# A decoder trunk on one core: the last unit of each down projection by column halves over both tiles, and what is ordered around it

## The reference, cut to what matters

```python
def rms_norm(x, g):
    y = xf * lax.rsqrt(jnp.mean(xf * xf, axis=-1, keepdims=True) + NORM_EPS)
    return (y * g).astype(x.dtype)

def modulate(x, g, shift, scale):
    return rms_norm(x, g) * (1 + scale[:, None, :]) + shift[:, None, :]

hh = modulate(x, norm_g[l, 0], mod[:, 0], mod[:, 1])
x = x + 0.5 * mod[:, 2, None] * swiglu(hh, ffn_w_gu[l, 0], ffn_w_d[l, 0])
hh = modulate(x, norm_g[l, 1], mod[:, 3], mod[:, 4])
...                                    # rglru_mixer in layer 0, diff_attn_mixer in layer 1
x = x + mod[:, 5, None] * m
hh = modulate(x, norm_g[l, 2], mod[:, 6], mod[:, 7])
x = x + 0.5 * mod[:, 8, None] * swiglu(hh, ffn_w_gu[l, 1], ffn_w_d[l, 1])
...
y = rms_norm(x, final_g)
```

## Time and profile before

| what | value |
|---|---|
| three runs | 2417.99, 2424.96 and 2431.77 us |
| median | 2424.96 us |
| the profiled execution, its own time | 2418.17 us |
| its span, first to last instruction | 2416.4 us |
| mean granted TensorE clock | 0.991 |
| PE, DVE, ACT busy | 96%, 41%, 32% |
| chain that ended last | PE 83%, DVE 8%, issue 5%, ACT 3% |

### The profile page before, as it was taken

One profiled execution on the slowest core, in us unless ns is written; L12 is line 12 of the kernel. 1 busy time (PEld: TensorE's weight loads), 2 busy tenths in 40 slices (PEclk: granted clock), 3 DMA queues, 4 the chain that ended last, 5 costly groups with the idle time before them and its releaser, 6 DMA issues.

```text
span 2416.4 us, 42067 instructions
## 1 busy us (share of the span) xinstructions
PE 2322.3 (96%) x18402; PEld 2195.2 (91%) x18402; DVE 984.6 (41%) x1643; ACT 772.2 (32%) x1069; POOL 160.9 (7%) x133
## 2 busy tenths in 40 slices
PE   5999999999999999999999999999788899999998
PEld 4999999989899999999999999999544499999998
DVE  5222232488642322327452322327466553222325
ACT  4221212367442121225442122125344533212122
POOL 0100000000011010000001000010000101001010
PEclk9999999999999999999999999999899999999999
DMA  8432343212332432432532333214499432222221
GB/s 343 157 124 99 145 157 136 97 40 96 142 155 74 155 139 89 153 127 91 210 150 101 141 147 150 88 64 155 163 418 417 173 139 87 88 88 80 80 78 66
DMA packets 64553, 338.38 MB, mean 140 GB/s; under 512 B 8050, under 2 KB 12274, under 8 KB 34930
## 3 DMA queue, kind: packets, MB, share of 16 engines
q1 hardware_dynamic: 61426, 330.97, 36.0%
q10 hardware_dynamic: 2944, 4.72, 0.5%
HBM read 328.44 MB, written 7.23 MB: 139 GB/s over the span
## 4 chain that ended last, share of the span: by engine, by line
PE 83%; DVE 8%; issue 5%; ACT 3%; DMA 1%; POOL 0%; SPq 0%; ACTq 0%; DVEq 0%; POOLq 0%
PE ps L496 45%; PE ps L499 22%; PE ps L508 3%; PE ps L510 3%; PE ps L509 3%; PE ps L473 2%; DVE w_lo L1385 1%; PE ps L768 1%; DVE xc L1674 1%; PE ps L757 1%; PE ps L800 1%; ACT w_hi L881 1%; DVE hf L1420 0%; DVE hs L1717 0%; ACT nt L1229 0%
## 5 line engine op out<-in xcount | busy, mean ns | idle before, releaser
L496 PE MATMUL ps<-hh_hi,w_hi 128*128 128x288 f32 x2912 | 816.2, 295 | 1.6 <-DVE w_lo L1385 1.6
L496 PE MATMUL ps<-hh_lo,w_hi 128*128 128x288 f32 x2912 | 816.1, 295 | 0.0
L499 PE MATMUL ps<-hh_hi,w_lo 128*128 128x288 f32 x2912 | 617.0, 292 | 0.0
L496 PEld LDWEIGHTS ps<-hh_hi,w_hi 128*128 128x128 f32 x2912 | 546.2, 188 | 5.4 <-issue 3.3
L496 PEld LDWEIGHTS ps<-hh_lo,w_hi 128*128 128x128 f32 x2912 | 546.5, 188 | 0.4
L1385 DVE TENSOR_TENSOR w_lo<-raw,w_hi 128x2048 fp32r<-128x2048 f32 x164 | 375.9, 2292 | 304.6 <-ACT w_hi L881 281.7
L499 PEld LDWEIGHTS ps<-hh_hi,w_lo 128*128 128x128 f32 x2912 | 466.5, 188 | 0.0
L496 PE MATMUL ps<-h_lo,w_hi 128*128 128x288 f32 x1536 | 430.8, 295 | 0.0
L496 PE MATMUL ps<-h_hi,w_hi 128*128 128x288 f32 x1536 | 429.9, 295 | 0.7 <-DVE x L1565 0.7
L881 ACT ACTIVATE w_hi<-raw 128x2048 fp32r<-128x2048 f32 x159 | 303.4, 1908 | 332.0 <-PE ps L499 317.8
L499 PE MATMUL ps<-h_hi,w_lo 128*128 128x288 f32 x1536 | 325.5, 292 | 0.0
(11 more groups left out here) (224 smaller groups left out, 1957.3 us busy)
## 6 DMA issues: line engine op xcount, KB each, us to landing
raw<-in_w_gu SPq DMA_DIRECT2D x88, 1024.0 KB, 4.8
ada<-in_ada_w SPq DMA_DIRECT2D x76, 1024.0 KB, 10.8
raw<-in_w_d SPq DMA_DIRECT2D x32, 1024.0 KB, 4.8
kr<-in_k_cache SPq DMA_DIRECT2D x64, 512.0 KB, 7.8
vr<-in_v_cache SPq DMA_DIRECT2D x64, 512.0 KB, 8.3
raw<-in_w_d SPq DMA_DIRECT2D x16, 768.0 KB, 4.3
raw<-in_w_in SPq DMA_DIRECT2D x8, 1024.0 KB, 5.0
raw<-in_w_kv SPq DMA_DIRECT2D x8, 1024.0 KB, 4.9
```

The source lines that it names most:

```text
L496: pe.matmul(ps[:, 2 * s + n, 0:TH], whi, r[:, k, TH * n:TH * n + TH], start=(k == 0 and r is rhs_hi), stop=False)
L499: mm = pe.matmul(ps[:, 2 * s + n, 0:TH], wlo, rhs_hi[:, k, TH * n:TH * n + TH], start=False, stop=(k == k_tiles - 1))
```

## The change

The last unit goes by column halves over both tiles: (half 0, tile 0), (half 0, tile 1), (half 1, tile 0), (half 1, tile 1). The sums of half 0 (`acc_sums`, then `last_sums`) stand ahead of the last three products of (half 1, tile 0); those of half 1 move behind the `ada_burst` of the next stage. The squares of block 6 are made and added by halves (`square_six`, `add_six`). DVE's `last_unit` does the first 288 columns of both residuals, the rest of block 6, then two norm blocks of the next stage (`norm_start`) or two final rows, and only then the rest of block 7. The remaining norm blocks are `norm_rest`.

```diff
             def unit_with_sums(u, j, kt, st):
...
-                tile_products(j, 0, h_hi, h_lo, 0, kt, None, 0, "out0_full")
-                pe.wait_ge(sems["s1_free"], u + CREDITS["s1_free"])
                 for n in range(2):
-                    for k in range(kt):
-                        mm = part(j, 1, n, k, h_hi, h_lo, kt)
-                        if n == 1 and k == kt - 2:
-                            acc_sums(st)
-                    mm.then_inc(sems["w_done" if n else "half_full"], 1)
-                last_sums(st, 0)
+                    for t in range(2):
+                        if (n, t) == (0, 1):
+                            pe.wait_ge(sems["s1_free"], u + CREDITS["s1_free"])
+                        for k in range(kt):
+                            mm = part(j, t, n, k, h_hi, h_lo, kt)
+                            if (n, t, k) == (1, 0, kt - 2):
+                                acc_sums(st, 0)
+                                last_sums(st, 0)
+                        mm.then_inc(sems[("out0_full", "w_done")[t] if n else "half_full"], 1)
...
@@ first_unit and first_pair @@
+                acc_sums(sums, 1)
                 last_sums(sums, 1)
...
@@ ScalarE, behind the units of a down projection @@
-                        act.wait_ge(sems["res_half"], s["stat"])
+                        act.wait_ge(sems["res_half"], 2 * s["stat"] - 1)
+                        square_six(s["stat"], 0)
+                        act.wait_ge(sems["res_half"], 2 * s["stat"])
                         square_half(s["stat"], 0)
                         statistics(s["stat"], 0)
+                        act.wait_ge(sems["s0_free"], u0 + s["units"] + CREDITS["s0_free"])
+                        square_six(s["stat"], 1)
+                        if not s["last"]:
+                            norm_first(plan[at + 1], 0, False, range(2))
                         act.wait_ge(sems["s1_free"], u0 + s["units"] + CREDITS["s1_free"])
                         square_half(s["stat"], 1)
...
@@ VectorE @@
+            def add_six(st, n):
+
+                cols = slice(TH * n, TH * n + TH)
+                dve.wait_ge(sems["sq6_full"], 2 * st + n - 1)
+                dve.wait_ge(sems["sq_sum"], 8 * st + KT - 1)
+                dve.tensor_tensor(rstd[:, cols], rstd[:, cols], sg[0][:, cols], ALU.add)\
+                   .then_inc(sems["sq_sum" if n else "sq6_sum"], 1)
+
+            def last_unit(s, u, norm):
+
+                st, res = s["stat"], s["res"]
+                for t in range(2):
+                    residual_first(u, KT - 2 + t, t, "half_full", 2 * st - 1 + t).then_inc(sems["res_half"], 1)
+                    if t == 0:
+                        add_six(st, 0)
+                residual_second(u, KT - 2, 0, res + KT - 2)
+                add_six(st, 1)
+                if norm:
+                    norm_start(norm)
+                else:
+                    final_rows(s, 0, range(2))
+                residual_second(u, KT - 1, 1, res + KT - 1)
```

More of the change, by code:

```diff
@@ L632, in unit, with acc_sums @@
                     ada_turn(BURSTS[u])
[L634 to L638, removed]
+            def acc_sums(st, n):
+                if st and n == 0:
+                    pe.wait_ge(sems["sq6_sum"], st)
+                else:
+                    pe.wait_ge(sems["sq_sum"], 8 * st + 8)
+                pe.matmul(ps[:, 6 + n, 0:TH], ones, rstd[:, TH * n:TH * n + TH], start=True, stop=False)
             def last_sums(st, n):
@@ L656, in _ @@
             pe.wait_ge(sems["cond_ready"], 1)
-            acc_sums(0)
             for n in range(2):
+                acc_sums(0, n)
                 last_sums(0, n)
@@ L725, in _ @@
                     if s["last"]:
+                        acc_sums(s["stat"], 1)
                         last_sums(s["stat"], 1)
@@ L940, in norm_hi, with norm_first @@
                                bias=mods[:, s["sh"] + k, 0:1]).then_inc(sems["norm_hi"], 1)
-            def norm_first(s, sums, freed):
+            def norm_first(s, sums, freed, blocks=range(KT)):
                 act.wait_ge(sems["ada_evac"], s["sh"] // 8 + 1)
-                for k in range(KT):
+                for k in blocks:
                     if freed and k < KT - 1:
@@ L1434, in after_kv, with norm_start, norm_rest @@
                 return s["norm"] and plan[plan.index(s) - 1]["kind"] == "kv"
+            def norm_start(s):
+                dve.wait_ge(sems["h_lo"], s["h"] + CREDITS["h_lo"])
+                dve.wait_ge(sems["rstd_ready"], 2 * s["stat"] - 1)
+                for k in range(2):
+                    norm_gain(s, 0, k)
+                for k in range(2):
+                    norm_low(s, 0, k)
+            def norm_rest(s):
+                dve.wait_ge(sems["s1_free"], s["u"] + CREDITS["s1_free"])
+                for k in range(2, 4):
+                    norm_gain(s, 0, k)
+                for k in range(4, KT):
+                    dve.wait_ge(sems["norm_lo"], 16 * s["norm"] + k - 3)
+                    norm_gain(s, 0, k)
+                    norm_low(s, 0, k - 2)
+                for k in range(KT - 2, KT):
+                    norm_low(s, 0, k)
             def norm_first(s):
@@ L1600, in _ @@
                 if s["kind"] == "final":
[L1601 to L1606, removed]
+                    final_rows(plan[at - 1], 0, range(2, KT))
+                    final_rows(plan[at - 1], 1, range(KT))
                 if s["kind"] == "up":
@@ L1640, in _ @@
                             modulation(plan[at + 1])
[L1641 to L1645, removed]
+                        if s["sums"] and m == s["units"] - 1:
+                            last_unit(s, u, None if s["last"] else plan[at + 1])
+                        else:
+                            for t in range(2):
+                                k = 2 * m + t
+                                residual(u, k, t, s["res"] + k)
+                                if s["sums"]:
+                                    add_square(s["stat"], k)
                         if u in BURSTS:
```

44 lines of the change are left out of this document (29 added, 15 removed).

## The result

The changed kernel takes 2424.08 us (median of 12 runs, 2422.19 to 2433.52), the kernel before 2420.1 us on the same chip (median of 12, 2417.99 to 2431.77). The ratio is 1.0018, 95% interval [1.0009, 1.0026]: 2 to 6 us slower, inside the 0.5% that were called "no change". A second set of runs of the same kernel gave 1.0022 [1.0010, 1.0033]. The forecast was 2427.8 on the older median of 2424.96, +2.8 us (+0.12%); the measured ratio is +0.18%. That older median, of three runs, lay 4.9 us above the median of twelve, so the differences are to be compared and not the 2427.8 itself. (In the later sets of runs one execution of each kernel took far longer, 3853 and 7489 us; the ratios leave these two out.)

A forecast was written before the change was run, and what follows sets the result against it. The prediction took PE, busy for 96% of the span, to bound the kernel. Its terms 3.25 + 0.8 + 1.34 - 1.4 - 1.2 gave +2.8 us on the median 2424.96, so 2427.8 us, range 2416 to 2436.

The forecast's parts named there:

- Boundary 1, +3.25: First stage change: PE stops at half 0's sums, tile 1's release and the burst come later, half 1 starts 3.25 us later.
- the predicted 1.3: At boundary 1, a new PE stop of 1.3 us at the sums of half 0.
- Boundaries 3 and 4, +0.67 each: Stage changes 3 and 4: the new stop gives back the won `w_lo` wait; half 1 starts 0.67 us later at each.
- Boundaries 2 and 5, -0.7: Stage changes with `kt` 8: no stop at the sums, and PE passes the `w_lo` wait 0.7 us earlier at each.
- the end, -1.2: Boundary 6: two of 16 final rows made ahead of the last residual, the other 14 start sooner; end 1.2 us earlier.
- The clock, +0.8 (0 to 1.6) at boundary 1: A half-clock stretch of PE after the new idle time ahead of the burst, taken as 0.8 us, between 0 and 1.6.
- The price of 1.5: Cost in us of one slow clock stretch on PE: 15 products in 3.30 us instead of 25 at 0.130.
- A: Block 6's residual and sums are in time everywhere, as a step ahead on DVE ends sooner; -7 us, 2418; chance 0.13.
- B: New PE stops at boundaries 1, 3 and 4 each bring a slow clock stretch; +6.5 us, 2431.5; chance 0.22.
- C: Waiting early sums and the earlier norm cancel, also at boundary 1, ACT's Ln coming earlier; 0 to -1, 2424.5; chance 0.15.

The follow-up runs named there:

- e1: The changed kernel with the first unit's burst issued ahead of its waits for `w_lo`, `s0_free` and `s1_free`; 2420.2 us in one run.
- e2: The changed kernel with the sums of half 0 moved 15 products later on PE in units of 6 blocks, not the last; 2425.13 us in one run.
- e3: The changed kernel with DVE's next `w_lo` and modulation moved from ahead of the last unit's first residual to behind block 6's half add; 2425.71 us in one run.
- e4: The changed kernel without the two early norm blocks; the norm of half 0 begins behind tile 1's release; 2421.33 us in one run.
- e5: The changed kernel with the first unit's burst ahead of its waits, and `w_lo` and modulation behind block 6's half add; 2417.43 us (median of 11), ratio 0.9989.
- e8: The changed kernel as it is, run a second time; 2425.12 us (median of 12), ratio 1.0022.
- e9: The changed kernel without its two early final rows, all 16 standing behind the last residual; 2428.03 us in one run.
- e6: The kernel before, with the first unit's burst issued ahead of its waits for `w_lo`, `s0_free` and `s1_free`; 2418.37 us in one run.

## Why the prediction was right, and where its sizes failed

**Boundary 1, +3.25 (measured +3.36): right, step by step.** The stop is 1.14 in the bracket and 1.30 from where the next product would have started (478.73) to the sums at 480.03, which is how the predicted 1.3 was counted; the burst is +2.88 (+2.77). The runs with the changed order add up in one way. The shift of half 1 is the shift of the burst, plus 0.48 for the two passes of the sums that now stand behind it, plus what a slow stretch takes on the burst itself (its length less 3.66):

| kernel | idle ahead of the burst | burst | slow stretch on it | sum with 0.48 | half 1, measured |
|---|---|---|---|---|---|
| changed | 2.46 | +2.88 | 0 | 3.36 | +3.36 |
| e1 | 0 | +0.36 | 0 | 0.84 | +0.84 |
| e2 | 4.05 | +2.65 | 2.86 | 5.99 | +5.99 |
| e3 | 3.11 | +1.80 | 1.65 | 3.93 | +3.94 |
| e4 | 1.09 | +1.52 | 0 | 2.00 | +2.00 |
| e5 | 0 | -1.38 | 0 | -0.90 | -0.90 |
| e8 | 2.45 | +2.88 | 1.69 | 5.05 | +5.05 |
| e9 | 2.45 | +2.87 | 1.69 | 5.04 | +5.04 |

So what the change does here it does through one instruction's place: the burst, which needs nothing from tile 1, waits for its release (e1, e4).

**Boundaries 3 and 4, +0.67 each (measured +0.91 and +0.92): the mechanism right, the term small by a quarter.** I had PE and `w_lo` ready at the same moment, 1124.4. PE's side was nearly so: the parts of half 0 came 1.51 later (1.4 predicted). What was too small is the Ln that `w_lo` follows, +0.65 in the prediction. Less the 3.86 us by which this execution is late when it reaches the boundary, it is +0.93 behind the earlier trace rows:

```profile
1122.57 0.48 ACT L941 ACTIVATE rstd<-ps,small 128x288 f32<-128x288 f32 x1
```

`w_lo` keeps its distance to it (3.65; 3.66 before) and lets half 1 go +0.92 late. The stop itself is not the cause, which I had not separated: e2 takes it away and wins 0.2. The cause is `w_lo` on DVE ahead of the first residual (e3: 1.07).

**Behind boundary 4, +0.57: a step that I left out.** The next stage is a q pair. ACT copies its swapped halves when PE has finished half 0 of the pair, 1.5 us later now, so ACT's L1017 is later and DVE waits 1.33 for it where it waited 0.76:

```profile
1683.64 0.69 DVE L1568 TENSOR_TENSOR hh_lo<-sg,hh_hi 128x512 fp32r<-128x512 f32 x1 [1.33 <-ACT hh_hi L1017]
```

PE shows it as a new stop behind DVE's `oT`:

```profile
1686.93 0.40 PE L508 MATMUL ps<-hh_hi,w_hi 128*128 128x288 f32 x1 [0.39 <-DVE oT L1513]
```

I stopped at `w_lo` and took the wait there as the boundary's end; the shift of half 0 had another customer.

**Boundaries 2 and 5, -0.7 (-0.78, -0.79), and the end, -1.2 (-1.33): right.** No stop at the sums, no wait for `w_lo`. At the end the two rows alone make half of it (e9).

**The clock, +0.8 (0 to 1.6) at boundary 1: the kind right, the size no trace's.** Behind the stop of 2.45 or 2.46 us the burst lost nothing in the first trace and 1.69 in e8 and in e9; the 0.8 lay between two such cases. That the first trace lost 0.75 near 509 instead is luck, not this term. (The price of 1.5 was a little more than its own rows give, 3.30 less 15 times 0.130, or 1.35; near 509 a stretch took 1.47.) What I left out altogether is that the one trace of before is itself a draw: slow stretches that stand there anyway, behind long waits in the recurrence and attention stages, cover more or less of PE's work from one execution to the next.

**The rivals.** A fell at boundaries 1, 3 and 4: the residual of block 6 is in time only when `w_lo` is moved behind it (e3). Its rule, in the Trainium skill's page "Perfetto Trace Analysis", section "Optimizing Scalar/DVE Operations", is that breaking up instructions of engines that aren't saturated may let work end sooner. The trace agrees at the boundaries of 8 blocks (-0.78) and at the end (-1.33), where no `w_lo` stands ahead, and not at boundaries 3 and 4 (+0.91), so DVE's busy share over the whole span (41%) doesn't tell where it holds. B fell in its place: the stops of 1.15 at boundaries 3 and 4 had no slow stretch behind them in any trace that has them. Its limit, an idle stretch between 1.60 and 2.23 us, doesn't show either (last section). At boundary 1 it holds in part: the grown stop ahead of the burst cost 1.69 in two of three traces. C fell with +3.36.

The timed +4.0 and +5.3 us (medians) lie between the boundaries' own +2.9 and the profiled +6.5. Which part of the 1.1 to 2.4 us above 2.9 belongs to the change (the stop ahead of its burst cost 1.69 in e8 and e9) and which to chance, the runs don't separate: e5, whose burst has no stop ahead of it, lies 1.4 to 1.8 above its own -4.1. So the cause of the boundaries' +2.9 is shown and that of the rest is open; and that the time fell into a range of 20 us says little about either.

## What to carry to other kernels

Work that needs nothing from the step ahead, like the burst here, should be issued ahead of the waits: behind them, each microsecond by which the chain grows is paid in full. Asking for a result earlier pays only if its maker's in-order queue can make it earlier; look at what stands ahead of the first instruction of the chain (here a 2.3 us `w_lo`), and move that together with the consumer. Taking away the stop that the consumer shows wins little (0.2 of 1.15 here) if the stop only covers the chain behind it.

## What was not expected of the hardware

Equal stops of PE are not equally followed by the 1.2 GHz level. Behind the stop of 1.60 to 1.62 us ahead of L496 (near 505), a half-clock stretch stands in the changed kernel's first trace, e1, e3 and e5, and none in the kernel before, e2, e4, e6, e8 and e9. Behind the idle 2.45 us ahead of the burst there is one in e8 and e9 and none in the first trace of the same order. Over all ten traces the burst ran partly at half clock in four of the five with 2.45 to 4.05 us of idle time ahead of it, and in none of the five with 1.09 or less. So a longer stop is more often followed by it, but a single trace can't price a stop's clock. The Trainium skill, page "TensorE: Matmul & The Clock Gate", section "What's actually happening", says that the gate's timing does not restart with the kernel and that the number of slow products differs from run to run; the two traces of the changed kernel agree, 0 against 1.69 us on one burst.
